# Two orders on the vector engine of a two-block transformer kernel: weight low halves before a rotated low half, and transposed probabilities' low halves before biased scores

## The reference

```python
def second_block(x, w_in, w_out, na_rpb, ...):
    h = rms_norm(x, norm_mix[l])
    proj = h @ w_in[l]
    na_q, na_k, na_v, r_q, r_k, r_v, r_g = jnp.split(proj, splits, axis=-1)
    na_out = neighbourhood_attention(na_q, na_k, na_v, na_rpb[l])   # 8 heads of 64
    rq = rotary(r_q, pos)                                           # 4 heads of 64
    rk = rotary(r_k, pos) * RET_QK_DIM ** -0.5
    ret = bidirectional_retention(rq, rk, r_v, ...)
    ...
    mix = jnp.concatenate([na_out, silu(r_g) * head_group_norm(ret)], axis=-1)
    x = x + mix @ w_out[l]
```

## Time and profile before

| | |
|---|---|
| median of 3 runs | 1303.32 us (1301.70 to 1304.52) |
| the profiled execution | 1304.54 us, its span 1302.7 us |
| TensorE busy | 1278.1 us, 98% of the span, 6086 matmuls |
| VectorE busy | 802.3 us, 62% |
| ScalarE busy | 634.5 us, 49% |
| GpSimd busy | 155.1 us, 12% |
| granted TensorE clock | 0.995 of full speed |

### The profile page before, as it was taken

How to read it: one execution, slowest core, us unless ns; L and a number is a source line. 1 busy time by engine, 2 the same in 40 slices (tenths; PEclk the granted TensorE clock), 3 DMA queues, 4 the chain that set the end, 5 groups by cost and what they waited for, 6 DMA issues and landing times.

```text
span 1302.7 us, 16590 instructions
## 1 busy us (share of the span) xinstructions
PE 1278.1 (98%) x6086; PEld 1062.3 (82%) x6086; DVE 802.3 (62%) x1553; ACT 634.5 (49%) x1239; POOL 155.1 (12%) x146
## 2 busy tenths in 40 slices
PE   8999999999999999999999999999999999999997
PEld 7888888868888888888788777888888888888886
DVE  5789799685654566346788886588644343344344
ACT  6687576454335443233455655476543242332343
POOL 0021120000010001000002101022311030110111
PEclk9999999999999999999999999999999999999998
DMA  7211110423332333332333222432333323233321
GB/s 266 85 46 41 42 41 18 157 76 90 99 97 71 115 104 97 98 90 81 113 90 89 89 57 64 128 105 77 91 96 97 94 76 114 81 113 97 98 81 65
DMA packets 64623, 118.19 MB, mean 91 GB/s; under 512 B 7712, under 2 KB 12192, under 8 KB 64288
## 3 DMA queue, kind: packets, MB, share of 16 engines
q1 hardware_dynamic: 62848, 112.95, 29.2%
q10 hardware_dynamic: 1696, 4.19, 1.0%
HBM read 115.02 MB, written 2.10 MB: 90 GB/s over the span
## 4 chain that ended last, share of the span: by engine, by line
PE 88%; DVE 7%; ACT 2%; issue 2%; DMA 1%; POOL 0%; SPq 0%; POOLq 0%; DVEq 0%; ACTq 0%
PE bank L581 26%; PE bank L583 26%; PE bank L582 25%; PE bank L781 2%; PE bank L662 2%; PE bank L664 2%; PE bank L663 2%; DVE pp L2094 1%; PE bank L767 1%; PE bank L768 1%; DVE ptl L2117 1%; DVE pp L2111 1%; PE bank L735 1%; DMA praw<-in_pT 0%; DVE qs L2010 0%
## 5 line engine op out<-in xcount | busy, mean ns | idle before, releaser
L1923 DVE TENSOR_TENSOR wl<-raw,wh 128x512 fp32r<-128x512 f32 (+2 forms) x360 | 265.9, 750 | 330.8 <-ACT wh L1257 330.1
L1257 ACT ACTIVATE wh<-raw 128x512 fp32r<-128x512 f32 (+1 forms) x398 | 242.3, 619 | 289.6 <-PE bank L583 276.0
L581 PE MATMUL bank<-AH,wh 128*128 128x512 f32 (+1 forms) x848 | 333.5, 393 | 0.9 <-DVE AL L1937 0.3
L583 PE MATMUL bank<-AH,wl 128*128 128x512 f32 (+1 forms) x848 | 329.2, 388 | 0.0
L582 PE MATMUL bank<-AL,wh 128*128 128x512 f32 (+1 forms) x848 | 326.9, 386 | 0.0
L581 PE MATMUL bank<-BH,wh 128*128 128x512 f32 x624 | 247.9, 397 | 1.3 <-DVE wl L1923 1.3
L583 PE MATMUL bank<-BH,wl 128*128 128x512 f32 x624 | 244.7, 392 | 0.0
L582 PE MATMUL bank<-BL,wh 128*128 128x512 f32 x624 | 243.2, 390 | 0.0
L583 PEld LDWEIGHTS bank<-AH,wl 128*128 128x128 f32 x848 | 159.3, 188 | 35.4
L581 PEld LDWEIGHTS bank<-AH,wh 128*128 128x128 f32 x848 | 159.8, 188 | 34.7 <-issue 4.1
L582 PEld LDWEIGHTS bank<-AL,wh 128*128 128x128 f32 x848 | 159.5, 188 | 33.1 <-issue 0.2
(11 more groups left out here) (317 smaller groups left out, 1627.0 us busy)
## 6 DMA issues: line engine op xcount, KB each, us to landing
raw<-in_w_dn SPq DMA_DIRECT2D x104, 256.0 KB, 2.7
raw<-in_w_gu SPq DMA_DIRECT2D x88, 256.0 KB, 2.6
raw<-in_w_up SPq DMA_DIRECT2D x64, 256.0 KB, 2.6
raw<-in_w_nsa SPq DMA_DIRECT2D x16, 256.0 KB, 2.7
raw<-in_w_pg SPq DMA_DIRECT2D x16, 256.0 KB, 2.6
raw<-in_w_naq SPq DMA_DIRECT2D x16, 256.0 KB, 2.6
nbi<-in_na_bias ACTq DMA_DIRECT2D x8, 448.0 KB, 3.4
raw<-in_w_swa SPq DMA_DIRECT2D x10, 256.0 KB, 2.7
```

What stands on the lines that cost most here:

```text
L581: t.matmul(o, w, xh, start=start, stop=False, skip_group_check=skip)
L583: return t.matmul(o, wl, xh, start=False, stop=stop, skip_group_check=skip)
L1257: a.activation(W[i % NW].h[:, 0:n], RAW[i % NRAW][:, 0:n], ACT.Copy).then_inc(*s_wh.up(i))
L1923: v.tensor_tensor(w.l[:, 0:n], RAW[i % NRAW][:, 0:n], w.h[:, 0:n], ALU.subtract).then_inc(*s_wl.up(i))
```

## The change

Only the order of DVE's list changes. No instruction is added, removed or altered, and the lists of the four other engines are the same.

```diff
@@ vector, rotation
             rotated(0)
+            behind("w_ret", 3)
+            ahead("w_ret", 4, 2)
             rotated_low(0)
             rotated(1)
-            behind("w_ret", 3)
-            ahead("w_ret", 4, 2)
             straight(2)
@@ vector, neighbourhood attention
             for s in range(10):
+                if s >= 2:
+                    u = s - 2
+                    rest(NA, ("na", u), PT2[u % 2], [s_pv.at(("na", u - 2))] if u >= 2 else [])
                 if s < 8:
                     ready = [s_nb[s % 2].at(s)] + ([s_tr.at((("na", s - 2), 2))] if s >= 2 else [])
                     soft(NA, ("na", s), PP2[s % 2], na_bias_of(s), -1.0, 3.0e38, M4[s % 6], *ready)
-                if s >= 2:
-                    u = s - 2
-                    rest(NA, ("na", u), PT2[u % 2], [s_pv.at(("na", u - 2))] if u >= 2 else [])
```

## The result

The changed kernel takes 1309.1 us (median of 5 runs, 1308.52 to 1311.08) against 1303.32 of the kernel before (1301.70 to 1304.75 in 5). The ratio is 1.0051 with the interval [1.0040, 1.0062], so it is slower by 5.2 to 8.1 us. The forecast was 1305.2, 1.9 us slower, and its range ended at 1307.6. The direction was right and the size too small by a factor of three.

The account below looks back on a forecast made before the run. TensorE, busy nearly all the time, was taken as the bound, with 2.6 us of waits to win. Attention +2.1 and rotation -0.2 gave +1.9 us, from the median 1303.32 to 1305.2 us; range 1302.0 to 1307.6.

Parts of the forecast that it names:

- What bounds the kernel: Whole kernel: TensorE is busy nearly always, so only its three waits, 2.6 us, can be won; DVE and ACT have little slack.
- Rotation: Rotation: the 1.3 us wait for a weight low half goes, the first `v_part` then waits for sdl, and 0.2 us stay.
- Closed chain: Attention loop: p2l ahead of `soft` closes a chain of 7.23 us a round against TensorE's 6.2; the attention costs 2.1 us.
- Collisions: Attention, steps 2 and 4: fourth low half of the keys starts near POOL's second piece; DVE reckoned first, so nothing lost.
- The first: Rival, attention: POOL is first and holds DVE, chain 1.3 us longer in step 2, 4 or both; say 1307.0 us; chance 0.2.
- The second: Rival: all three waits go and the delay of `soft` is hidden; 2.6 us less, 1300.7 us; chance 0.1.
- The third: Rival, a wash: rotation keeps most of its 1.3 us or the chain is shorter, gains and costs cancel; 1303.3 us; chance 0.2.
- the double collision: Attention: DVE held by POOL in both step 2 and step 4, the chain 1.3 us longer in each; outside the range.

Follow-up runs that it names:

- rot_only: The kernel before with only the rotation's half of the change: ratio 0.9999 [0.9990, 1.0008].
- after_held: The changed kernel with POOL's pieces beside the keys or queries made to wait until DVE has written that step's low half of the output: ratio 1.0013.
- att_only: The kernel before with only the attention's half of the change: ratio 1.0061 [1.0048, 1.0075].
- att_5to7: The kernel before with p2l ahead of `soft` only in steps 5, 6 and 7, rotation as before: ratio 1.0014.
- after_hold_q: The changed kernel with POOL held back only beside the low halves of the queries in DVE's step 3: ratio 1.0042.
- before_met: The kernel before, DVE's order kept, POOL's pieces of steps 2 to 4 made to start with the first low half of the keys or queries: ratio 1.0037.

## Why the prediction was right or wrong

**What bounds the kernel: right.** TensorE's waits are the quantity. That DVE and ACT have little slack in the attention was right too, and was taken too lightly: it is why nothing that was lost in steps 2 to 4 came back.

**Rotation: right.** The wait for wl goes, 1.1 us come back at `v_part`, and 0.2 us were to stay: 0.19 in `rot_only` (13.28 - 13.09).

**Closed chain: right in mechanism, 0.4 us short.** `after_held`, without meetings, has `soft` of units 2 to 7 late by 1.90, 2.12, 2.63, 2.55, 3.26, 3.77 where the prediction has 1.93, 2.22, 2.56, 2.55, 3.01, 3.53, and rounds of 7.48 and 7.22 us where it has 7.23. The second bank of the scores of unit 6, expected 1.45 us late, is 1.37 late there (34.18 against 32.81 from the start of A):

```profile
882.99 0.44 PE L767 MATMUL bank<-nka,nq 128*128 128x384 f32 x1 [1.21 <-DVE small L2094]
```

The values of unit 6 are 2.24 us late against 1.83. Of the missing 0.4, `soft` of unit 7 has 0.24 (3.77 against 3.53). The weight loads that are no longer done ahead behind each new wait may be part of it; no run shows how much.

**Collisions: here the step failed.** The term for meetings of DVE with POOL was put at nothing in the sum. The prediction said that the fourth low half of the keys starts "within some 0.2 us of POOL's second piece (about 861.9)", and went on: "If DVE is first, as I reckon, nothing is lost". Counted from the same start, the fourth starts at 861.92 and POOL's second piece at 861.79: the place was right to a few hundredths, and POOL was first by 0.13 us. Four things were wrong in what followed from it.
- A tie was given to one side, with 0.2 for the other. The row of four starts when the first has been let go by POOL and follows at 0.71 us, while ACT's list puts POOL's second piece 3.14 us after the first (855.87 to 859.01): this is no accident of one step, and step 4 has the same 0.13.
- "Nothing is lost" left out the first meeting of the row. It ends 0.67 us late and AL has 0.30 us of slack there. Without the second meeting AL of step 2 would have started 11.98 us behind the start of A, by an estimate (860.88 - 1.02 - 847.88), against 11.56 in `after_held`: some 0.4 us lost in step 2 and in step 4 even with the tie won.
- The queries of step 3 were not in the account at all. Their pieces on POOL are 1.83 us apart (867.66 to 869.49), with two low halves of DVE between, and each meets one.
- So the price was 1.43, 1.32 and 1.40 us in three steps, 4.15 in all, where the sum had nothing and the rival had 1.3 in step 2, in step 4 or in both.

**The clock: not in the account.** 7.10 - 2.35 - 4.15 leaves 0.60 us for A, 0.10 of it for the meeting of step 8. That the clock is the cause of most of the rest is argued from the rounds: 7.99 us from `soft` 5 to `soft` 6 against 7.48 in `after_held`, and 8.42 in `att_only`, with the same delay of `soft` 5 and the lower clock for longer. This is less than the 1.57 us that a fall of this size cost in B. TensorE was busy for 1.53 us more in A than in `after_held` (56.47 against 54.94), but it also waited for DVE there, so not all of that became time. No run held the clock up with the waits in place, so its share isn't measured by itself.

**The rivals.** The first is what happened, in both steps that it named and in step 3 besides, and its sign came: the fourth low half of the keys took 1.71 and 1.69 us. It had a chance of 0.2. The second (the waits go and the delay is hidden) is excluded by the wait for the bank of `soft`, 1.21 us in `after_held`, and by `att_5to7`, in which nothing else is at work and A still grows. Its argument was also misread: TensorE has two filling pieces in steps 0 to 3 and one in step 4, not two in steps 2 to 4. The third had a gain of the rotation that wasn't there. The range left out the double collision; what came was more than that.

## What to carry to other kernels

Moving an instruction by 2 us on an engine moves everything behind it against the other engines' pieces. Before such a move, lay the shifted list beside that of the engine it can be held by, and count every pair that would overlap, not only the first (here DVE's instructions with two SBUF inputs and POOL's pieces; `norm`'s scaling, with one tile and a column, was held too, 1.84 us instead of 1.28). A predicted tie of a tenth of a us should be priced as if it may be lost: the starts here were forecast to a few hundredths, and the side was still wrong. And before an instruction is moved forward to end a wait, ask who waits for what it is moved past: here the waits for p2l shrank and came back as waits for a bank or for the scaled probabilities.

## What the runs showed of the hardware

- Two meetings in one row. A DVE instruction with two SBUF inputs that starts 0.1 to 0.5 us after a POOL piece ends 0.54 or 0.55 us behind that piece (1.36, 1.71, 1.36, 1.69 us instead of 0.69). The instructions queued behind it then follow at 0.71 us, and so the fourth of a row can meet the next piece. The Trainium skill, SBUF — State Buffer, section "Who interferes with whom", says that issue order decides who blocks. The traces agree: 0.13 us decided over 1.0 us here. But the held instruction is not put off by its whole 0.69 us: it ends 0.55 behind POOL's end and not 0.69. And in the kernel before, POOL's piece at 861.20 began 0.13 us ahead of the end of a low half of the keys (860.64 + 0.69) and took its usual 1.30.
- Being first helps one instruction and not the row. In `before_met` DVE's first low half began 0.04 us before POOL's piece and took 0.69 us, POOL's piece took 1.79 instead of 1.29, and DVE's second low half took 1.68: both sides lost in the same meeting.
- Behind two waits of TensorE of 2.67 and 1.47 us, with four matmuls between, the granted clock fell to its lower level of 1.2 GHz for some 4 us (0.55, 0.59, then 1.00). With 1.2 us of wait in one place, in `after_held`, it stayed at 1.00. In B of `after_hold_q` it fell as far (0.57, 0.58) with no wait near, and that cost 1.57 us.
- An idle time of 0.19 us on TensorE was a delay of 0.58 us, through the shown length of the matmul before it and the weight load that is no longer done ahead.
